# Expert outputs of a two-layer trunk: low halves taken by TensorE and ScalarE, gates moved to the hidden values

## What is computed

```python
def swiglu(t, w_gate, w_up, w_down):
    return (jax.nn.silu(t @ w_gate) * (t @ w_up)) @ w_down

def moe_swiglu(x, w_router, w_gate, w_up, w_down):
    ...
    top_vals, top_idx = lax.top_k(logits, TOP_K)          # TOP_K = 2 of N_EXPERTS = 8
    top_w = jax.nn.softmax(top_vals, axis=-1)
    gates = jnp.sum(jax.nn.one_hot(top_idx, N_EXPERTS) * top_w[..., None], axis=1)
    for e in range(N_EXPERTS):
        out = out + gates[:, e:e + 1] * swiglu(t, w_gate[e], w_up[e], w_down[e])
```

## Time and profile before

| | |
|---|---|
| median of three runs | 1165.77 us (1165.61 to 1586.93) |
| profiled execution, its own time | 1165.15 us |
| its span, first to last instruction | 1163.3 us |
| the experts, about | 700 to 1150 us of the span |
| PE, DVE, ACT busy over the whole span | 1131.7, 874.0, 758.3 us |

### The profile page before, as it was taken

One profiled execution on the slowest core, in us unless ns is written; L12 is line 12 of the kernel. 1 busy time (PEld: TensorE's weight loads), 2 busy tenths in 40 slices (PEclk: granted clock), 3 DMA queues, 4 the chain that ended last, 5 costly groups with the idle time before them and its releaser, 6 DMA issues.

```text
span 1163.3 us, 15755 instructions
## 1 busy us (share of the span) xinstructions
PE 1131.7 (97%) x5580; PEld 948.8 (82%) x5580; DVE 874.0 (75%) x990; ACT 758.3 (65%) x936; POOL 23.2 (2%) x59
## 2 busy tenths in 40 slices
PE   8999999999999999999999999999899999999996
PEld 7887788888888888887788888888768888888884
DVE  5567666666554455467666679999999999999997
ACT  5556566545444445555566546789889987888785
POOL 3000000000000001000001000000000000000000
PEclk9999999999999999999999999999999999999998
DMA  8845522659555344645523655999999999999993
GB/s 297 298 136 183 170 74 82 215 186 322 181 181 193 131 167 145 208 136 183 170 74 98 215 191 201 403 388 406 407 407 407 407 406 403 366 403 389 408 372 135
DMA packets 120555, 294.96 MB, mean 254 GB/s; under 512 B 9007, under 2 KB 33677, under 8 KB 119965
## 3 DMA queue, kind: packets, MB, share of 16 engines
q1 hardware_dynamic: 119376, 288.66, 68.9%
q0 software_dynamic: 960, 5.28, 1.3%
q10 hardware_dynamic: 140, 0.04, 0.0%
HBM read 292.90 MB, written 1.05 MB: 253 GB/s over the span
## 4 chain that ended last, share of the span: by engine, by line
PE 51%; issue 42%; ACT 3%; DVE 2%; DMA 1%; SPq 0%; POOL 0%; POOLq 0%; ACTq 0%; DVEq 0%
PE bank L1612 16%; PE bank L1613 15%; PE bank L1614 15%; PE bank L1650 2%; ACT w_hi L677 1%; DMA raw<-in_w_in 1%; PE bank L1813 1%; PE bank L1793 1%; ACT p_buf L811 1%; DVE mixed L1294 1%; PE bank L1801 1%; PE bank L1785 1%; DVE small L1297 1%; ACT pT L817 1%; PE bank L1849 0%
## 5 line engine op out<-in xcount | busy, mean ns | idle before, releaser
L1075 DVE TENSOR_TENSOR w_lo<-raw,w_hi 128x1536 fp32r<-128x1536 f32 (+3 forms) x144 | 242.9, 1692 | 174.0 <-ACT w_hi L677 173.5
L677 ACT ACTIVATE w_hi<-raw 128x1536 fp32r<-128x1536 f32 (+4 forms) x144 | 205.6, 1433 | 157.4 <-PE bank L1614 155.9
L1389 DVE TENSOR_TENSOR w_lo<-raw,w_hi 128x1792 fp32r<-128x1792 f32 (+3 forms) x148 | 286.5, 1965 | 12.2 <-ACT w_hi L866 11.9
L866 ACT ACTIVATE w_hi<-raw 128x1792 fp32r<-128x1792 f32 (+3 forms) x148 | 244.4, 1669 | 48.7 <-PE bank L1614 33.7
L1612 PE MATMUL bank<-w_hi,aT_hi 128*128 128x512 f32 (+1 forms) x592 | 235.2, 397 | 0.7 <-DVE w_lo L1075 0.5
L1614 PE MATMUL bank<-w_hi,aT_lo 128*128 128x512 f32 (+1 forms) x592 | 229.9, 388 | 0.0
L1613 PE MATMUL bank<-w_lo,aT_hi 128*128 128x512 f32 (+1 forms) x592 | 229.6, 388 | 0.0
L1612 PEld LDWEIGHTS bank<-w_hi,aT_hi 128*128 128x128 f32 x592 | 111.3, 188 | 23.0 <-DVE w_lo L1075 1.5
L1614 PEld LDWEIGHTS bank<-w_hi,aT_lo 128*128 128x128 f32 x592 | 111.1, 188 | 22.5
L1613 PEld LDWEIGHTS bank<-w_lo,aT_hi 128*128 128x128 f32 x592 | 111.4, 188 | 20.3
L1389 DVE TENSOR_TENSOR w_lo_more<-raw,w_hi_more 128x1792 fp32r<-128x1792 f32 (+3 forms) x50 | 96.7, 1941 | 4.4 <-ACT w_hi_more L866 4.4
(11 more groups left out here) (317 smaller groups left out, 1791.3 us busy)
## 6 DMA issues: line engine op xcount, KB each, us to landing
raw<-in_moe_w_gate SPq DMA_DIRECT2D x128, 448.0 KB, 7.4
raw<-in_moe_w_up SPq DMA_DIRECT2D x128, 448.0 KB, 7.1
raw<-in_moe_w_down SPq DMA_DIRECT2D x112, 512.0 KB, 7.2
raw<-in_w_in SPq DMA_DIRECT2D x40, 768.0 KB, 4.4
raw<-in_dense_w_gate SPq DMA_DIRECT2D x22, 512.0 KB, 4.0
raw<-in_dense_w_up SPq DMA_DIRECT2D x22, 512.0 KB, 4.8
raw<-in_dense_w_down SPq DMA_DIRECT2D x11, 1024.0 KB, 5.0
raw<-in_w_in SPq DMA_DIRECT2D x20, 512.0 KB, 4.8
```

What stands on the lines that cost most here:

```text
L677: act.activation(w_hi[:, weight_slot(b, j), 0:n], raw[:, b % 2, j, 0:n], ACT.Copy).then_inc(hi_made[j], 1)
L866: act.activation(split_of(hi_slot, m), raw_of(i, n), ACT.Copy).then_inc(e_hi_made, 1)
L1075: dve.tensor_tensor(w_lo[:, s, 0:n], raw[:, b % 2, j, 0:n], w_hi[:, s, 0:n].bitcast(F32), ALU.subtract).then_inc(lo_made[j], 1)
L1389: dve.tensor_tensor(split_of(lo_slot, m), raw_of(i, n), split_of(hi_slot, m).bitcast(F32), ALU.subtract).then_inc(e_lo_made, 1)
```

## The change

For experts 0 to 6 the subtraction moves from VectorE to TensorE and ScalarE. TensorE multiplies y_hi by a negative identity and accumulates it onto the same bank (`take_high_off`, two matmuls of 512 columns, behind granule 4 of step 2e + 3), so that the bank holds bank - y_hi; ScalarE copies that to y_lo (`output_rest`, two copies at granule 5). The last expert still has the subtraction on VectorE, as a plain `tensor_tensor`. The gate is no longer multiplied into the output but into the hidden values, in the instruction on VectorE that multiplies silu by up, which becomes a `scalar_tensor_tensor` and now waits for `gate_in`; `output_hi` becomes a copy without a scale and without that wait. A tile `minus_ident_r` is made once on VectorE.

```diff
             def output_hi(r, e):
-                act.wait_ge(gate_in, PAIRS_E * r + e // 2 + 1)
                 ...
-                    act.activation(y_of[e % 2][0][:, u * NB:(u + 1) * NB], bank[B_Y[u]][:, :], ACT.Copy,
-                                   scale=slot_gate[:, e // 2 % 2, e % 2:e % 2 + 1]).then_inc(y_hi_made, 1)
+                    act.activation(y_of[e % 2][0][:, u * NB:(u + 1) * NB], bank[B_Y[u]][:, :], ACT.Copy).then_inc(y_hi_made, 1)
+
+            def output_rest(r, e):
+                for u in range(2):
+                    act.wait_ge(y_rest, 2 * ((EXPERTS - 1) * r + e) + u + 1)
+                    act.activation(y_of[e % 2][1][:, u * NB:(u + 1) * NB], bank[B_Y[u]][:, :], ACT.Copy).then_inc(y_lo_made, 1)
@@
+                    if n == 5 and k % 2 and 1 < k < STEPS:
+                        output_rest(r, k // 2 - 1)
@@
+                    dve.tensor_scalar(minus_ident_r[:, :], ident[:, :], -1.0, None, ALU.mult).then_inc(ones_made, 1)
@@ output_lo
-                    dve.scalar_tensor_tensor(out=lo_of[:, part], in0=bank[B_Y[u]][:, :], scalar=slot_gate[:, e // 2 % 2, e % 2:e % 2 + 1],
-                                             in1=hi_of[:, part].bitcast(F32), op0=ALU.mult, op1=ALU.subtract).then_inc(y_lo_made, 1)
+                    dve.tensor_tensor(lo_of[:, part], bank[B_Y[u]][:, :], hi_of[:, part].bitcast(F32), ALU.subtract).then_inc(y_lo_made, 1)
@@ expert_hidden
+                p, x = k // 4, k % 4 // 2
+                dve.wait_ge(gate_in, PAIRS_E * r + p + 1)
                 ...
-                    dve.tensor_tensor(hid_buf[0:rows, part], sg_buf[0:rows, part], bank[B_UP[u]][0:rows, 0:HN],
-                                      ALU.mult).then_inc(e_hid_made, 1)
+                    dve.scalar_tensor_tensor(out=hid_buf[0:rows, part], in0=bank[B_UP[u]][0:rows, 0:HN], scalar=slot_gate[0:rows, p % 2, x:x + 1],
+                                             in1=sg_buf[0:rows, part], op0=ALU.mult, op1=ALU.mult).then_inc(e_hid_made, 1)
@@
-                    if n == GU_N + HK - 1 and k % 2 == 0:
-                        output_lo(EXPERTS * r + k // 2 - 1)
+                    if (k, n) == (STEPS, GU_N + HK - 1):
+                        output_lo(EXPERTS * (r + 1) - 1)
@@
+            def take_high_off(r, e):
+                for u in range(2):
+                    pe.wait_ge(y_hi_made, 2 * (EXPERTS * r + e) + u + 1)
+                    pe.matmul(bank[B_Y[u]][:, :], minus_ident_r[:, :], y_of[e % 2][0][:, u * NB:(u + 1) * NB],
+                              start=False, stop=True, skip_group_check=True).then_inc(y_rest, 1)
@@
+                        if n == 4 and k % 2 and 1 < k < STEPS:
+                            take_high_off(r, k // 2 - 1)
```

More of the change, by code:

```diff
@@ L274, in build_trunk @@
             [("y1_hi", [P, D], F32R), ("y1_lo", [P, D], F32R)])
-        (proj, zT, q, k, v, sg_buf, hid_buf, hT_hi_buf, hT_lo_buf, rt, fold, sel, selT, slot_no, token_slot, chosen, tri, ones, tri_r, ones_r, counts, flag, iota_i, shift, ident_r, key, key_base, top, order, rank_of, moved, slot_sorted, gate_sorted, slot_gate, _, ang, turns, rowc, row0, pos_i, posf, freq) = regions(
+        (proj, zT, q, k, v, sg_buf, hid_buf, hT_hi_buf, hT_lo_buf, rt, fold, sel, selT, slot_no, token_slot, chosen, tri, ones, tri_r, ones_r, counts, flag, iota_i, shift, ident_r, minus_ident_r, key, key_base, top, order, rank_of, moved, slot_sorted, gate_sorted, slot_gate, _, ang, turns, rowc, row0, pos_i, posf, freq) = regions(
             [("proj", [P, 3, NT, D]), ("zT", [P, KC, S])],
@@ L285, in build_trunk @@
              ("tri", [P, P]), ("ones", [P, P]), ("tri_r", [P, P], F32R), ("ones_r", [P, P], F32R), ("counts", [P, 8]), ("flag", [P, 1], I32), ("iota_i", [P, ROUNDS * P], I32),
-             ("shift", [P, P], F32R), ("ident_r", [P, P], F32R), ("key", [P, EXPERTS]), ("key_base", [P, EXPERTS]), ("top", [P, EXPERTS]), ("order", [P, EXPERTS], I32),
+             ("shift", [P, P], F32R), ("ident_r", [P, P], F32R), ("minus_ident_r", [P, P], F32R), ("key", [P, EXPERTS]), ("key_base", [P, EXPERTS]), ("top", [P, EXPERTS]), ("order", [P, EXPERTS], I32),
              ("rank_of", [P, EXPERTS, EXPERTS]), ("moved", [P, NT, EXPERTS, EXPERTS]), ("slot_sorted", [P, NT, EXPERTS]),
@@ L339, in build_trunk @@
             "gu_made", "silu_made", "hid_made", "hid_tr", "hT_hi_made", "hT_lo_made", "h_new"))
-        xn_hi_made, xn_lo_made, chosen_made, ranks_made, iota_made, flag_made, sel_made, x_hi_tr, x_lo_tr, x_hi_in, x_lo_in, selT_tr, selT_in, y_hi_made, y_lo_made, back_made = (
+        xn_hi_made, xn_lo_made, chosen_made, ranks_made, iota_made, flag_made, sel_made, x_hi_tr, x_lo_tr, x_hi_in, x_lo_in, selT_tr, selT_in, y_hi_made, y_rest, y_lo_made, back_made = (
             sem(n) for n in ("xn_hi_made", "xn_lo_made", "chosen_made", "ranks_made", "iota_made", "flag_made", "sel_made", "x_hi_tr", "x_lo_tr",
-                             "x_hi_in", "x_lo_in", "selT_tr", "selT_in", "y_hi_made", "y_lo_made", "back_made"))
+                             "x_hi_in", "x_lo_in", "selT_tr", "selT_in", "y_hi_made", "y_rest", "y_lo_made", "back_made"))
         e_raw_in = [sem(f"e_raw_in{s}") for s in range(RAW_SLOTS)]
@@ L1504, in output_lo @@
             def output_lo(E):
-                e = E % EXPERTS
-                hi_of, lo_of = y_of[e % 2]
+                hi_of, lo_of = y_of[E % 2]
                 for u in range(2):
@@ L1920, in _ @@
             keep_busy(1, 14)
-            pe.wait_ge(ones_made, 5)
+            pe.wait_ge(ones_made, 6)
             pe.wait_ge(chosen_made, 1)
```

## The result

The changed kernel takes 1170.19 us (median of 6 runs, 1169.43 to 1171.32) against 1165.69 us before; the ratio is 1.0045, with a 95% interval of 1.0036 to 1.0055. By the ratio it is slower by 5.2 us (4.2 to 6.4), by the two medians 4.5 us; that is well within 2% and within the range of the prediction, but above its number, 1168.6 us. One of the six executions of the kernel before took 1586.93 us; the ratio is taken from the fast executions alone and leaves it out. The profiled execution took 1169.43 us, 4.3 us more than that of before, at the same granted clock of 0.997.

A forecast was written before the change was run, and what follows sets the result against it. Transfers bound the kernel where experts are small, PE where large, ScalarE behind experts 0, 4 and 6. Terms summed to +2.8 us on the profiled 1165.15, giving 1167.95, plus 0.6 for the median: 1168.6 us, range 1164.0 to 1172.0.

The forecast's parts named there:

- Experts 0 and 1: About 785 and 840 us: DMA at its limit sets the pace, so holding ScalarE and PE costs 0.
- Expert 2: Behind 898.05 us: ScalarE's split slips 0.95 us, pauses absorb 0.4, so VectorE and PE are late by about 0.5 us.
- Expert 3: Step 9, where PE is full: PE's two added matmuls cost 0.5 us.
- Expert 4: From 1005.69 us: full ScalarE delays VectorE, then PE, whose own 0.5 us vanish in its wait; 0.8 us lost.
- Expert 5: Step 13, where PE is full: PE's added matmuls cost 0.5 us.
- Expert 6: From about 1119.9 us: VectorE starts earlier, then waits for ScalarE 0.4 us; longer hidden products add 0.1; 0.5 us lost.
- Tail: Program end: PE adds the residual during the last y_lo, so shorter y_hi and y_lo gain nothing; 0.
- The expected signs: Profile after: no y_hi bracket before take-off matmuls, ScalarE 10.00 at 1020 to 1030 us, more VectorE waits, DMA share unchanged.
- a sign against it: y_hi of expert 4 earlier than before would mean VectorE set the pace; forecast was 1.0 us late against 1005.69 us.
- All hidden: Rival: ScalarE's pauses move and later requests find DMA ahead; -1.2 to +1.2 us, 1164.6 to 1167.0 us; chance 0.25.
- VectorE as the pace: Rival: VectorE's relief lets transfers start earlier behind expert outputs; 1157 to 1164 us, likeliest 1163; chance 0.15.
- TensorE stalling for y_hi: Rival: PE stands still at granule 4, 1 to 3 us at each of seven places; 1171 to 1186 us; chance 0.10.

The follow-up runs named there:

- e7: The changed kernel with its end written in line on VectorE and ScalarE, so no jump over skipped rounds precedes it: 1167.90 us, ratio 1.0029.
- e9: The changed kernel with the low part taken by TensorE and ScalarE for experts 0 to 2 only, VectorE subtracting for the others: 1164.76 us, ratio 1.0001.
- e2: The changed kernel without TensorE's 14 matmuls on minus_ident_r, so y_lo repeats the high part; ScalarE's copies stay: 1167.82 us, ratio 1.0027.
- e1: The kernel before with gates moved into the hidden values; VectorE still subtracts for y_lo, as a plain tensor_tensor: 1164.60 us, ratio 0.9995.
- e6: The kernel before with the gates' move alone, and its end in line on VectorE and ScalarE without the jump: 1163.94 us, ratio 0.9996.
- e12: The changed kernel with the take-off for experts 4 and 6 only, plus 11 never-executed instructions in VectorE's skipped rounds: 1167.66 us, ratio 1.0025.
- e10: The changed kernel with the low part taken by TensorE and ScalarE for experts 3 to 6 only: 1167.58 us, ratio 1.0022.
- e11: The changed kernel with the low part taken by TensorE and ScalarE for experts 4 and 6 only: 1168.07 us, ratio 1.0026.

## Why the prediction was right and where it failed

**The sum among the experts was right, 2.8 us against 2.68 (2.35 to 3.12 in the four executions with this work, e7's +2.55 among them).** Term by term:

- *Experts 0 and 1: nothing.* Right within a scatter of 0.5 us; e9 shows 0.1 us for experts 0 to 2 by its ratio.
- *Expert 2: 0.5.* Wrong, -0.09 to +0.15. The step that failed is "0.4 us I take" for what ScalarE's pauses absorb: they took all of it. From its y_hi, at 890.37 us against 891.28, to the next nothing was lost.
- *Expert 3: 0.5 by TensorE's work.* 0.29 to 0.45; the pair measured 0.46.
- *Expert 4: 0.8.* 1.14 to 1.20. The step that failed is "PE's own 0.5 us disappear in the wait". Without the matmuls it is 0.83, what ScalarE's copies cost, and with them 1.14: some 0.3 of the 0.5 us come on top. They come through ScalarE. Its copy of the hidden values (L971) waits for TensorE's transposes, which stand behind the take-off. In e2 it follows the split before it at once, 6.57 us behind the start of y_hi:

```profile
1004.08 1.09 ACT L983 ACTIVATE y_hi<-bank 128x512 fp32r<-128x512 f32 x2 [1.01 <-PE bank L1620]
...
1010.65 0.58 ACT L971 ACTIVATE hT_hi_buf<-bank 128x448 fp32r<-128x448 f32 x1
```

  In the kernel after it starts 6.89 us behind y_hi (1012.23 against 1005.34 us), with the bracket [0.15 <-PE bank L1994] shown further up, and what ScalarE does in the next 16 us is 0.33 us later too. I had followed the chain from ScalarE to TensorE and not back. TensorE's wait near 1031 us, in which the 0.5 us should have disappeared, is as long as in the earlier trace rows:

```profile
1032.08 0.48 PE L1618 MATMUL bank<-w_hi_more,xT 128*128 128x448 f32 x1 [0.43 <-DVE w_lo_more L1395]
```

- *Expert 5: 0.5.* 0.56 to 0.60, of which 0.1 to 0.2 is there with the gates' edit alone (e1, e6, e9), which the forecast did not put here.
- *Expert 6: 0.5.* 0.70 in every kernel that has both parts. e2 shows 0.45 without the matmuls, so they add 0.26 here, and the term lacked them. The way is the same: the copies to y_lo start 6.17 us behind y_hi in e2 and 6.43 us in the kernel after. VectorE's own part came as forecast. It starts its splits 2.7 us behind y_hi, not 2.95 us, and later waits for ScalarE where in the earlier trace rows it ran through (kernel after):

```profile
1121.39 5.89 DVE L1395 TENSOR_TENSOR w_lo<-raw,w_hi 128x1792 fp32r<-128x1792 f32 x3 [0.81 <-ACT w_hi L866]
...
1130.26 4.23 DVE L1395 TENSOR_TENSOR w_lo<-raw,w_hi 128x1792 fp32r<-128x1792 f32 x2 [0.43 <-ACT w_hi L866]
1134.70 2.29 DVE L1395 TENSOR_TENSOR w_lo<-raw,w_hi 128x2048 fp32r<-128x2048 f32 x1 [0.21 <-ACT w_hi L866]
```

  The 0.81 us stand where its subtractions stood; the forecast had the next 0.4 us and not the last 0.2.

- *Tail: 0.* This step failed, and it is more than the whole of the difference between the forecast and the result. In the profiled execution, 1169.43 us against 1167.95, that is 1.5 us: 2.3 more in the end, 0.1 less among the experts and 0.6 less ahead of them. I weighed y_hi and y_lo there and not the jump that stands right behind them. The end is 2.3 us longer, and 41 unexecuted instructions take those 2.3 us away. Nothing in the lists of work foretells it; it hangs on the number of instructions in VectorE's program. By what mechanism is inferred, not shown.

Errors of +0.4 at expert 2 and -0.6 at 4 and 6 cancelled, so the total looks better than its parts. The expected signs came as said: no brackets in front of the take-off, ScalarE at 10.00 between 1020 and 1030 us, the DMA share from 730 us at 1.03, and VectorE's wait moved to ScalarE. y_hi of expert 4 came 0.35 us earlier than before, which the prediction had named as a sign against it; but this execution was 0.6 us ahead already at y_hi of expert 0, before the first take-off (e1 to e12 as well, by 0.1 to 0.8 us), and from there on it lost. Counted from y_hi of expert 0, those of experts 4 and 6 are late by 0.3 and 2.0 us, where 1.0 and 2.3 were forecast; of the 0.7 us missing at expert 4 half is the term of expert 2 and most of the rest the scatter of the first two columns. Absolute starts were a poor test; differences between neighbours are the better one.

**The rivals.** All hidden is wrong for experts 3 to 6 and right for 0 to 2. VectorE as the pace: VectorE's relief came out as 8.4 us of waiting for ScalarE, and no stage gained. The Trainium skill's rule (Perfetto Trace Analysis, Identifying the Most-Contended Engine: improve the engine with the highest occupancy first) would have picked VectorE among the compute engines, with 10.00 of 10 in 860 to 870 us. The measured time doesn't bear it out: one of the engines that took over its work, ScalarE, was the one that it waited for. TensorE stalling for y_hi: no bracket at any of the 14.

No version beat the kernel before. Gates alone, with or without the end in line, are at 0.9995 and 0.9996, with intervals that hold 1.

## What to carry to other kernels

Before moving work off a busy engine, ask which engine that one waits for, and don't move it there: here 8.3 us of relief became 8.4 us of waiting. Price the same edit place by place; it was free where transfers set the pace, cost TensorE's work where TensorE was full, and cost ScalarE's work and a part of TensorE's where ScalarE was full. A wait of TensorE further on does not hide new matmuls if the engine that it waits for needs something that TensorE makes right behind them. When two versions differ by a few microseconds, look behind each taken jump for an idle time on "issue", and try the slower one with a few unexecuted instructions before its time is put down to the work.

## What the runs showed of the hardware

- Instructions that are never executed moved the end by 2.3 us: behind a taken jump VectorE stood idle for 5.51 us with none of them and for 3.17 us with 12 or 41. With no jump on VectorE and ScalarE it was 1.79 us. The difference is almost as large as what the change costs elsewhere.
- In all twelve kernels with the jump the long idle times, and only those, have a fourth 8 KB instruction packet ahead of their end. Which place of the code calls for it is open (e10, e11 and e12 have idle times of 3.52, 4.63 and 4.59 us).
- The profile can name a releaser (ScalarE's hg, 4.59 us) that had been done 1.7 us before.
- On 448 columns `scalar_tensor_tensor` takes 0.065 us more than `tensor_tensor`. A copy of 512 columns from PSUM takes 575 to 597 ns without a scale and 681 ns with one from a tile.
